# The four score maps of a differential-attention half: PSUM layout and order of their matmuls

## The chip, the cores and the metric

One core of a Trainium2 chip runs the whole program in one launch. The metric is the time of one execution in microseconds of the device (us); lower is better. The kernel's engines are TensorE (PE; its weight loads are listed as PEld), VectorE (DVE), ScalarE (ACT), GpSimd (POOL) and the DMA queues (issued from SyncE, SP).

## The reference

The program is two transformer blocks, two layers each, on 256 tokens of width 1024. Each layer is a feed-forward part, a token mixer and a second feed-forward part. The change lies in the token mixer of the first block, which joins four mixers of four heads each; only differential attention is touched:

```python
def diff_attention(q, k, v, ..., cos, sin):        # 2*DIFF_HEADS = 8 maps, DIFF_DH = 32
    q = apply_rope(q.reshape(bsz, seq, 8, 32), cos, sin)
    k = apply_rope(k.reshape(bsz, seq, 8, 32), cos, sin)
...
        scores = jnp.einsum('bhqd,bhkd->bhqk', q_blk, kt)
        allowed = key_chunk[None, :] <= q_chunk[:, None]      # chunks of 64 tokens
        p = jax.nn.softmax(jnp.where(allowed, scores, -jnp.inf), axis=-1)
        p = p.reshape(bsz, 4, 2, Q_BLOCK, seq)
        return jnp.einsum('bhqk,bhkd->bhqd', p[:, :, 0] - lam * p[:, :, 1], vt)
```

So eight score maps are needed in each of two layers. For the first 128 queries only the first 128 keys can be allowed, for the second 128 all 256: a map is 128 queries by 128 + 256 = 384 keys, with a contraction over 32.

## The kernel before

Each engine has a hand-written order of work, and they meet through counting semaphores: `after(S, name)` waits until the step `name` of the list `S` is done, `then_inc(S.done(name), 1)` counts it. `T1` are TensorE's steps of the mixer, `V1` VectorE's, `A1` ScalarE's.

Every weight matrix is used as a pair of a rounded part and a rest (`w_hi`, made by ScalarE in line 198; `w_lo`, made by VectorE in line 205), in units of 1024 columns, of which three can be held. The mixer of the first block has 16 projections (`project(n)`, lines 229 to 235 and 306 to 312 multiply them), and between them, and halfway through them, TensorE does the small products of the four mixers. One such string of work is a block-wise triangular inverse of twelve steps: `update(i)` (lines 1167 and 1168), then `product(i + 1)` (line 1156) on TensorE, `subtracted(i)` (line 1667) and `masked(i + 1)` (line 1661) on VectorE.

The eight maps are made in two calls, `maps(0)` and `maps(1)`, four maps each. The operand `dqk` holds the 32 features of map j on partitions 32j to 32j + 31, so each matmul uses a quarter of the array's rows, given by `tile_position=(32 * j, 0)`. In PSUM (`ps`, 8 banks of 512 floats) maps 0, 1 and 2 lie in banks 3, 4 and 5, columns 0 to 383 each; map 3 is cut into three pieces of 128 that lie in columns 384 to 511 of the same three banks. Maps 0 to 2 are issued without a wait between them; map 3 waits for the step `map{c}2`. All of this is float32, and a float32 matmul is two passes, each with a weight load and a matmul record in the trace.

TensorE's order is: `update(1)`, `product(2)`, `maps(0)`, first half of projection 9, then `step_2` (`update(2)`, `product(3)`, a wait for `mask_d0`, the row products `rows_m` in line 953), and so on; later `update(3)`, `product(4)`, `maps(1)`, projection 10 with `step_4` halfway (`update(4)`, `product(5)`, a wait for `mask_d1`, the head scores of line 1143, whose two halves `qk_m_even` and `qk_m` also have a wait between them).

On VectorE `masked_maps(c)` waits for `map{c}3`, adds the mask `NEGD` in two instructions while copying the maps from PSUM to `dS` (lines 1681 and 1682), takes the row maxima (line 1686) and scales them (line 1689). ScalarE's `softmax_exp(c)` (line 1472) follows. Then VectorE goes on with `subtracted(2)` or `subtracted(4)`.

Of the kernel before, what the change touches and what calls it, by code (L numbers as in the profile page):

```python
# [22 lines left out]
ALU = mybir.AluOpType  # L23
# [3 lines left out]
P = 128  # L27
SEQ = 256
# [73 lines left out]
def over(ap, shape, *dims):  # L102

    for d in dims:
        ap = ap.unsqueeze(d)
    return ap.to_broadcast(shape)


def build(nc, t, out):
# [8 lines left out]
    def steps(name, names):  # L118
        return Steps(sem(name), names)


    ps = ctx.enter_context(nc.psum_tensor("ps", [P, 8, 512], F32))
# [817 lines left out]
    def scores_T(bank, kT_s, qT_t, h):  # L940

        nc.tensor.matmul(ps[:, bank, 0:SEQ], kT_s[:, 0:P], qT_t[:, 0:SEQ], start=True, stop=True)
        return nc.tensor.matmul(ps[:, bank, SEQ:SEQ + P], kT_s[:, P:SEQ], qT_t[:, P:SEQ], start=True, stop=True)

    def weighted_values(out0, out1, pT, v0, v1):

        nc.tensor.matmul(out0, pT[:, 0:P], v0, start=True, stop=True)
        nc.tensor.matmul(out1, pT[:, P:SEQ], v0, start=True, stop=False)
        return nc.tensor.matmul(out1, pT[:, SEQ:SEQ + P], v1, start=False, stop=True)
# [10 lines left out]
    def diag(buf):  # L960

        return buf[:].rearrange("p h (b n) -> p h b n", b=3)[:, :, 0:3:2, :]
# [72 lines left out]
    dS = m.take(8, 384)  # L1035
# [3 lines left out]
    dqk = rope_in.rearrange("p a (i n) -> p (a i) n", i=2)  # L1039
# [6 lines left out]
    def K(c, n=P):  # L1046
        return con[:, c - NBASE:c - NBASE + n]

    BLOCKS, NEGM, NEGD = K(C_BLOCK), K(C_NEGM), K(C_NEGD, 384)
# [7 lines left out]
    T1 = steps("mix1_t", "narrow sums rows_n kk_even kk qk_even qk x0 rope_t rows_a map00 map01 map02 map03 rows_m map10 map11 "  # L1057
                         "map12 map13 qk_m_even qk_m o_m trans_d vt rows_s xt_s o_d cb o_s u1 l21 transA u2 o_g transB "
                         "transC")
# [48 lines left out]
    def mixer1_pe(pe, B, l, g):  # L1108
        def after(S, name):
            pe.wait_ge(S.sem, S.at(name, l))  # L1110
# [74 lines left out]
            last.then_inc(T1.done(name), 1)  # L1185

        def maps(c):


            for j in range(4):  # L1190
                part = slice(32 * j, 32 * j + 32)
                keys = ((0, slice(0, P)), (P, slice(0, SEQ))) if j < 3 else ((0, slice(0, P)), (P, slice(0, P)), (P, slice(P, SEQ)))
                at = 0
                if j == 3:
                    after(T1, f"map{c}2")
                for i, (t_, s_) in enumerate(keys):
                    o = ps[:, 3 + j, at:at + s_.stop - s_.start] if j < 3 else ps[:, 3 + i, 384:512]
                    at += s_.stop - s_.start
                    last = nc.tensor.matmul(o, dqk[part, c, t_:t_ + P], dqk[part, 2 + c, s_], start=True, stop=True,
                                            tile_position=(32 * j, 0))  # L1200
                last.then_inc(T1.done(f"map{c}{j}"), 1)

        def mix_T(name):
# [102 lines left out]
        for c in range(4):  # L1306
            for tile in range(TILES):
                o = 32 + tile * 8 + 2 * c
                last = nc.tensor.matmul(ps[:, 5, o:o + 2], pm_sq[:, c, tile * P:(tile + 1) * P], BLOCKS[:, 0:P:64],
                                        start=True, stop=True)  # L1310
# [26 lines left out]
        for c in range(4):  # L1337
            for tile in range(TILES):
                o = (c % 2) * SEQ + tile * P
                last = nc.tensor.transpose(ps[:, 3 + c // 2, o:o + P], qkr[:, tile, c * P:(c + 1) * P], IDENT)  # L1340
# [4 lines left out]
        product(2)  # L1345
        after(V1, "mf")
        maps(0)
        project(9, step_2)

        update(3)  # L1350
        product(4)
        after(V1, "dec_m")
        maps(1)
        project(10, step_4)

# [4 lines left out]
        for h in range(H):  # L1360
            last = weighted_values(ps[:, 3, h * 65:(h + 1) * 65], ps[:, 4, h * 65:(h + 1) * 65], dT2[:, h, :],
                                   v_m[:, 0, h, :], v_m[:, 1, h, :])
# [7 lines left out]
        for h in range(H):  # L1370
            for b in range(3):
                last = nc.tensor.transpose(ps[:, 3 + b, h * P:(h + 1) * P], pD[:, h, b * P:(b + 1) * P], IDENT)
# [13 lines left out]
        for grp in range(2):  # L1386
            last = scores_T(3 + grp, cv[:, 8 + grp, :], cv[:, 10 + grp, :], grp)
# [4 lines left out]
        for h in range(H):  # L1392
            last = nc.tensor.matmul(ps[:, 4, h * 64:(h + 1) * 64], lT[:, h, P:SEQ], uu[:, 0, h * 64:(h + 1) * 64],
                                    start=True, stop=True)
# [7 lines left out]
        for h in range(H):  # L1402
            c = slice(h * 64, (h + 1) * 64)
            last = weighted_values(ps[:, 4, h * 64:(h + 1) * 64], ps[:, 4, SEQ + h * 64:SEQ + (h + 1) * 64],
                                   dT[:, h, :], uu[:, 0, c], uu[:, 1, c])
# [237 lines left out]
    def mixer1_dve(v, B, l):  # L1643
        def after(S, name):
            v.wait_ge(S.sem, S.at(name, l))
# [31 lines left out]
        def masked_maps(c):  # L1677

            after(T1, f"map{c}3")
            mine = slice(4 * c, 4 * c + 4)  # L1680
            nc.vector.tensor_tensor(dS[:, 4 * c:4 * c + 3, :], ps[:, 3:6, 0:384], over(NEGD, [P, 3, 384], 1), ALU.add)
            nc.vector.tensor_tensor(dS[:, 4 * c + 3, :].rearrange("p (b n) -> p b n", b=3), ps[:, 3:6, 384:512],
                                    NEGD.rearrange("p (b n) -> p b n", b=3), ALU.add).then_inc(V1.done(f"mask_d{c}"), 1)
            after(V1, f"mask_d{c}")
            for tile, part in enumerate((slice(0, P), slice(P, 384))):
                last = nc.vector.reduce_max(rmax[:, tile, mine], dS[:, mine, part], AX)
            last.then_inc(V1.done(f"max_d{c}"), 1)
            after(V1, f"max_d{c}")
            nc.vector.tensor_scalar(rmax[:, :, mine], rmax[:, :, mine], -(32.0 ** -0.5), None,
                                    ALU.mult).then_inc(V1.done(f"nmax_d{c}"), 1)  # L1690
# [119 lines left out]
        for g_ in range(2):  # L1810
            last = nc.vector.tensor_tensor(X[:, g_, 1, :].rearrange("p (h b n) -> p h b n", h=2, b=2),
                                           diag(lT)[:, 2 * g_:2 * g_ + 2, :, :], over(K(C_MT), [P, 2, 2, P], 1, 1), ALU.mult)
        last.then_inc(V1.done("mt1"), 1)
        after(V1, "mt1")
        for g_ in range(2):
            x4 = X[:, g_, 1, :].rearrange("p (i n) -> p i n", i=4)
            last = nc.vector.scalar_tensor_tensor(x4, x4, -1.0, over(IDENT, [P, 4, P], 1), ALU.mult, ALU.add)
# [9 lines left out]
        for h in range(H):  # L1827
            last = nc.vector.tensor_tensor(sq_m[:, 2 * h:2 * h + 2, :],
                                           ps[:, 3 + h // 2, (h % 2) * SEQ:(h % 2 + 1) * SEQ].rearrange("p (a n) -> p a n", a=2),
                                           over(NEGM, [P, 2, P], 1), ALU.add)  # L1830
# [15 lines left out]

        nc.vector.tensor_scalar(negm, negm, -1.0, 85.0, ALU.mult, ALU.min).then_inc(V1.done("negm"), 1)
        masked_maps(0)
        step(2)
        lo(10, (1,))  # L1850
        after(T1, "rows_m")
        decays(3, 0, dT2, acol, ALU.subtract, ALU.max).then_inc(V1.done("dec_m"), 1)
        step(3)
        lo(11, (0,))
        masked_maps(1)
        step(4)
        lo(11, (1,))
# [31 lines left out]
        for tile, part in enumerate((slice(0, P), slice(P, 384))):  # L1889
            w = part.stop - part.start  # L1890
            last = nc.vector.tensor_tensor(pD[:, :, part], dS2[:, :, 0, part], over(coef[:, tile, 0:8:2], [P, H, w], 2),
                                           ALU.mult)
            last = nc.vector.tensor_tensor(dS2[:, :, 1, part], dS2[:, :, 1, part], over(coef[:, tile, 1:8:2], [P, H, w], 2),
                                           ALU.mult)
# [29 lines left out]
        for grp in range(2):  # L1924
            last = nc.vector.tensor_tensor(dT2[:, 2 * grp:2 * grp + 2, :], over(ps[:, 3 + grp, 0:384], [P, 2, 384], 1),
                                           dT2[:, 2 * grp:2 * grp + 2, :], ALU.mult)
# [72 lines left out]
    part = m2.take(2, SEQ)  # L1999
# [814 lines left out]
```

## Time and profile before

| | |
|---|---|
| median of 3 runs | 2212.68 us (2207.97 to 2214.05) |
| the profiled execution | 2214.05 us, span of its instructions 2212.3 us |
| granted TensorE clock, mean | 0.995 |
| TensorE matmul busy | 2159.8 us, 98% of the span |
| VectorE busy | 1651.9 us, 75% |
| ScalarE busy | 1182.0 us, 53% |
| GpSimd busy | 67.2 us, 3% |
| DMA | 202 GB/s mean |

Busy shares are averages over stages with different limits. Which engine ends last in the mixer is read from the chain of waits and from the timeline of that stage. The profiled execution is the slowest of the three runs, so its sums stand 1.37 us above the median.

### The profile page before, as it was taken

How to read it: one execution, taken by the hardware profiler on the slowest of the kernel's cores; microseconds unless marked ns; L12 is line 12 of the kernel's file. 1: busy time of each engine (PE TensorE's matmuls, PEld its weight loads, DVE VectorE, ACT ScalarE, POOL GpSimd, SP SyncE). 2: the span in 40 equal slices, each digit the busy share in tenths (PEclk: the TensorE clock that was granted, in tenths of full speed). 3: DMA queues.
4: the chain of work that ended last, by engine and by line, in shares of the span. 5: the costliest groups of instructions: out<-in, count | busy, mean ns of one | idle time of the engine just before them, and what ended most of it. 6: DMA issues, size and time to landing. Idle time of an engine off the chain costs nothing.

```text
span 2212.3 us, 34936 instructions
## 1 busy us (share of the span) xinstructions
PE 2159.8 (98%) x13038; PEld 1898.1 (86%) x13038; DVE 1651.9 (75%) x2135; ACT 1182.0 (53%) x1589; POOL 67.2 (3%) x70
## 2 busy tenths in 40 slices
PE   8999999999999999999999999999999999999997
PEld 7888999888888889978888888998888888898886
DVE  6876797778678777867877777768787657766657
ACT  5455535554655573455446546556556545646554
POOL 0000200000000002000000000100000000100000
PEclk9999999999999999999999999999999999999999
DMA  8765322477487642217775775436764555434453
GB/s 308 294 266 210 115 77 95 191 275 286 153 329 270 255 153 96 77 58 286 283 270 211 277 280 203 153 115 235 297 244 174 190 207 209 153 115 152 171 192 150
DMA packets 59414, 446.68 MB, mean 202 GB/s; under 512 B 6976, under 2 KB 7360, under 8 KB 8896
## 3 DMA queue, kind: packets, MB, share of 16 engines
q1 hardware_dynamic: 59328, 445.50, 54.1%
q8 instruction: 59, 0.97, 0.2%
q14 instruction: 27, 0.22, 0.0%
HBM read 444.42 MB, written 1.05 MB: 201 GB/s over the span
## 4 chain that ended last, share of the span: by engine, by line
PE 88%; DVE 6%; ACT 3%; issue 1%; DMA 1%; SPq 0%; DVEq 0%; ACTq 0%
PE ps L248 28%; PE ps L357 15%; PE ps L253 14%; PE ps L363 7%; PE ps L264 3%; PE ps L306 2%; PE ps L307 2%; PE ps L312 2%; PE ps L338 1%; PE ps L229 1%; PE ps L235 1%; PE ps L230 1%; DVE w_lo L205 1%; PE ps L1156 1%; PE ps L1168 1%
## 5 line engine op out<-in xcount | busy, mean ns | idle before, releaser
L205 DVE TENSOR_TENSOR w_lo<-raw,w_hi 128x1024 fp32r<-128x1024 f32 x670 | 812.5, 1233 | 299.7 <-ACT w_hi L198 299.2
L198 ACT ACTIVATE w_hi<-raw 128x1024 fp32r<-128x1024 f32 x670 | 693.9, 1052 | 412.4 <-PE ps L363 133.1
L248 PE MATMUL ps<-hT,w_hi 128*128 128x512 f32 x2688 | 671.3, 392 | 0.1
L248 PEld LDWEIGHTS ps<-hT,w_hi 128*128 128x128 f32 x2688 | 487.9, 189 | 91.0 <-ACT w_hi L198 0.7
L253 PEld LDWEIGHTS ps<-hT,w_lo 128*128 128x128 f32 x2688 | 366.7, 190 | 26.2
L253 PE MATMUL ps<-hT,w_lo 128*128 128x256 f32 x2688 | 374.8, 282 | 0.0
L357 PE MATMUL ps<-w_hi,act_hi 128*128 128x512 f32 x672 | 209.9, 394 | 0.0
L357 PE MATMUL ps<-w_hi,act_lo 128*128 128x512 f32 x672 | 208.3, 391 | 0.0
L363 PE MATMUL ps<-w_lo,act_hi 128*128 128x512 f32 x672 | 179.7, 389 | 0.0
L2048 DVE SCALAR_TENSOR_TENSOR arena<-arena,cond 128x1024 f32<-128x1024 f32 x144 | 168.4, 1219 | 2.3 <-DMA arena<-in_w_ada 2.3
L357 PEld LDWEIGHTS ps<-w_hi,act_lo 128*128 128x128 f32 x672 | 126.7, 189 | 27.7
L363 PEld LDWEIGHTS ps<-w_lo,act_hi 128*128 128x128 f32 x672 | 126.3, 188 | 26.3
L357 PEld LDWEIGHTS ps<-w_hi,act_hi 128*128 128x128 f32 x672 | 121.2, 190 | 20.3
L306 PE MATMUL ps<-w_hi,hT 128*128 128x256 f32 x544 | 137.5, 290 | 0.0
L307 PE MATMUL ps<-w_hi,hT 128*128 128x256 f32 x544 | 133.9, 284 | 0.0
L461 ACT ACTIVATE arena<-ps 128x512 f32<-128x512 f32 x88 | 52.6, 598 | 139.1 <-PE ps L363 117.5
L448 ACT ACTIVATE act_hi<-hidden 128x512 fp32r<-128x512 f32 x80 | 50.5, 631 | 126.3 <-DVE hidden L511 126.3
L508 DVE TENSOR_TENSOR hidden<-ps,arena 128x512 f32<-128x512 f32 x88 | 60.8, 691 | 71.6 <-ACT arena L461 71.5
L306 PEld LDWEIGHTS ps<-w_hi,hT 128*128 128x128 f32 x544 | 104.7, 192 | 1.4 <-issue 0.7
L307 PEld LDWEIGHTS ps<-w_hi,hT 128*128 128x128 f32 x544 | 104.8, 193 | 0.0
L491 DVE TENSOR_TENSOR act_lo<-hidden,act_hi 128x512 fp32r<-128x512 f32 x80 | 55.3, 692 | 55.8 <-ACT act_hi L448 55.8
L453 ACT ACTIVATE arena<-ps 128x512 f32<-128x512 f32 x88 | 52.7, 599 | 78.9 <-PE ps L253 68.8
(364 smaller groups left out, 2535.0 us busy)
## 6 DMA issues: line engine op xcount, KB each, us to landing
raw<-in_u SPq DMA_DIRECT2D x88, 1024.0 KB, 4.9
raw<-in_d SPq DMA_DIRECT2D x88, 1024.0 KB, 6.8
raw<-in_g SPq DMA_DIRECT2D x87, 1024.0 KB, 4.9
arena<-in_w_ada SPq DMA_DIRECT2D x48, 1536.0 KB, 7.5
raw<-in_w_in SPq DMA_DIRECT2D x54, 1024.0 KB, 4.9
raw<-in_w_out SPq DMA_DIRECT2D x16, 1024.0 KB, 4.8
rows<-in_rows SPq DMA_DIRECT2D x12, 1024.0 KB, 9.0
arena<-in_con SPq DMA_DIRECT2D x1, 1344.0 KB, 11.1
```

Of the source, the lines that this page charges most:

```text
L198: nc.scalar.activation(w_hi[:, buf, 0:width], raw[:, slot, half * UNIT:half * UNIT + width], ACT.Copy).then_inc(unit_hi, 1)
L205: nc.vector.tensor_tensor(w_lo[:, buf, 0:width], raw[:, slot, half * UNIT:half * UNIT + width], w_hi[:, buf, 0:width].bitcast(F32), ALU.su ...
L248: nc.tensor.matmul(o, h_[:, k, c], hT[:, :, 4 * half + k, :], start=(half == k == 0), stop=False)
L253: last = nc.tensor.matmul(ps[:, bank + s, 0:SEQ], l_[:, k, c], hT_hi[:, 4 * half + k, :], start=False, stop=(half == 1 and k == 3))
L264: last = nc.tensor.matmul(place(s, z), w[:, k, s * P:(s + 1) * P], hT[:, end, 4 * j + k, :], start=start and k == 0 and (banks == 2 or s = ...
L306: nc.tensor.matmul(o, hT_hi[:, 4 * half + k, c], h_[:, k, :], start=(half == tile == k == 0), stop=False)
L307: nc.tensor.matmul(o, hT_lo[:, 4 * half + k, c], h_[:, k, :], start=False, stop=False)
L357: nc.tensor.matmul(ps[:, 2 * tile + half, :], part[:, c], w_hi[:, buf, half * 512:(half + 1) * 512], start=start and i == 0, stop=False)
L363: last = nc.tensor.matmul(ps[:, 2 * tile + half, :], left[0][:, c], w_lo[:, buf, half * 512:(half + 1) * 512], start=False, stop=stop)
L491: nc.vector.tensor_tensor(home[:, 0:FB // P, :].rearrange("p s t -> p (s t)"), act, hi[:, 0:FB // P, :].rearrange("p s t -> p (s t)").bitc ...
L508: nc.vector.tensor_tensor(out_, in_, part, ALU.add).then_inc(up_sum, 1)
L2048: last = nc.vector.scalar_tensor_tensor(block, block, 1.0, cond[:], ALU.mult, ALU.mult, accum_out=modc[:, n, b:b + 1] if k is first_chunk ...
```

## The change

Map by map, the pieces get another place in PSUM and another order. The 128-column pieces of all four maps (first 128 queries) lie side by side in bank 3. The 256-column pieces (second 128 queries) lie two to a bank in banks 4 and 5. Each map is now two matmuls, also map 3, and each map but the first waits for the one before it. On VectorE the mask is still added in two instructions, now one over the 4 x 128 columns of bank 3 and one over the 4 x 256 columns of banks 4 and 5.

```diff
         def maps(c):
             for j in range(4):
                 part = slice(32 * j, 32 * j + 32)
-                keys = ((0, slice(0, P)), (P, slice(0, SEQ))) if j < 3 else ((0, slice(0, P)), (P, slice(0, P)), (P, slice(P, SEQ)))
-                at = 0
-                if j == 3:
-                    after(T1, f"map{c}2")
-                for i, (t_, s_) in enumerate(keys):
-                    o = ps[:, 3 + j, at:at + s_.stop - s_.start] if j < 3 else ps[:, 3 + i, 384:512]
-                    at += s_.stop - s_.start
-                    last = nc.tensor.matmul(o, dqk[part, c, t_:t_ + P], dqk[part, 2 + c, s_], start=True, stop=True,
-                                            tile_position=(32 * j, 0))
+                if j:
+                    after(T1, f"map{c}{j - 1}")
+                nc.tensor.matmul(ps[:, 3, j * P:(j + 1) * P], dqk[part, c, 0:P], dqk[part, 2 + c, 0:P],
+                                 start=True, stop=True, tile_position=(32 * j, 0))
+                last = nc.tensor.matmul(ps[:, 4 + j // 2, (j % 2) * SEQ:(j % 2 + 1) * SEQ], dqk[part, c, P:SEQ],
+                                        dqk[part, 2 + c, :], start=True, stop=True, tile_position=(32 * j, 0))
                 last.then_inc(T1.done(f"map{c}{j}"), 1)
...
             after(T1, f"map{c}3")
             mine = slice(4 * c, 4 * c + 4)
-            nc.vector.tensor_tensor(dS[:, 4 * c:4 * c + 3, :], ps[:, 3:6, 0:384], over(NEGD, [P, 3, 384], 1), ALU.add)
-            nc.vector.tensor_tensor(dS[:, 4 * c + 3, :].rearrange("p (b n) -> p b n", b=3), ps[:, 3:6, 384:512],
-                                    NEGD.rearrange("p (b n) -> p b n", b=3), ALU.add).then_inc(V1.done(f"mask_d{c}"), 1)
+            nc.vector.tensor_tensor(dS[:, mine, 0:P], ps[:, 3, :].rearrange("p (j n) -> p j n", j=4),
+                                    over(NEGD[:, 0:P], [P, 4, P], 1), ALU.add)
+            nc.vector.tensor_tensor(dS[:, mine, P:384].rearrange("p (b j) n -> p b j n", b=2),
+                                    ps[:, 4:6, :].rearrange("p b (j n) -> p b j n", j=2),
+                                    over(NEGD[:, P:384], [P, 2, 2, SEQ], 1, 1), ALU.add).then_inc(V1.done(f"mask_d{c}"), 1)
```

## Rows read from the trace of the kernel before

**Rows 1.** The page's chain of work that ended last, by engine.
```profile
PE 88%; DVE 6%; ACT 3%; issue 1%; DMA 1%; SPq 0%; DVEq 0%; ACTq 0%
```

**Rows 2.** Line 1199 over the span: durations in ns; then who it waited for (us, times).
```profile
L1199 PE MATMUL ps<-arena x72: 270/372/377, 281.0 to 880.8; 32*128 32x128 f32 x48, 32*128 32x256 f32 x24
  PE ps L1199: 2.2, 4
```

**Rows 3.** Timeline of PE, first call, windows of different width: start, length, instructions.
```profile
280.95 0.40 PE L1199 MATMUL ps<-arena 32*128 32x128 f32 x3
...
281.17 0.52 PE L1199 MATMUL ps<-arena 32*128 32x128 f32 x6
...
281.28 0.62 PE L1199 MATMUL ps<-arena 32*128 32x256 f32 x6
...
281.50 0.40 PE L1199 MATMUL ps<-arena 32*128 32x256 f32 x3
...
282.05 0.93 PE L1199 MATMUL ps<-arena 32*128 32x128 f32 x6
282.91 0.39 PE L306 MATMUL ps<-w_hi,hT 128*128 128x256 f32 x1
```

**Rows 4.** Timeline of PEld, first call, at map 3; idle before it in brackets.
```profile
282.05 0.18 PEld L1199 LDWEIGHTS ps<-arena 32*128 32x128 f32 x1 [0.55 <-PE ps L1199]
```

**Rows 5.** Timeline of PE, the second call, and the fourth with what follows it.
```profile
296.00 2.02 PE L1199 MATMUL ps<-arena 32*128 32x128 f32 x18
...
879.04 2.02 PE L1199 MATMUL ps<-arena 32*128 32x128 f32 x18
880.99 0.39 PE L229 MATMUL ps<-hT,w_hi 128*128 128x256 f32 x1
```

**Rows 6.** Timeline of PE, two narrow windows about the wait inside the head scores.
```profile
305.04 0.27 PE L1143 MATMUL ps<-arena 64*128 64x128 f32 x1
...
305.37 0.37 PE L1143 MATMUL ps<-arena 64*128 64x128 f32 x1
```

**Rows 7.** Timeline of VectorE about the first call's maps.
```profile
281.31 0.68 DVE L1661 TENSOR_TENSOR hidden<-ps,arena 128x512 f32<-128x512 f32 x1
...
283.58 1.35 DVE L1681 TENSOR_TENSOR arena<-ps,arena 128x1152 f32<-128x1152 f32 x1
...
284.85 0.55 DVE L1682 TENSOR_TENSOR arena<-ps,arena 128x384 f32<-128x384 f32 x1
...
287.88 1.22 DVE L1667 TENSOR_TENSOR arena<-arena,ps 128x1024 f32<-128x1024 f32 x1 [0.42 <-PE ps L1168]
```

**Rows 8.** Timeline of PE: the products that ask for the masked maps, both calls.
```profile
288.57 1.95 PE L953 MATMUL ps<-base,arena 128*128 128x128 f32 x16
...
303.71 3.26 PE L1143 MATMUL ps<-arena 64*128 64x128 f32 x24
```

**Rows 9.** Timeline of VectorE about the second call's maps.
```profile
299.86 1.34 DVE L1681 TENSOR_TENSOR arena<-ps,arena 128x1152 f32<-128x1152 f32 x1
301.12 0.54 DVE L1682 TENSOR_TENSOR arena<-ps,arena 128x384 f32<-128x384 f32 x1
...
311.85 1.22 DVE L1667 TENSOR_TENSOR arena<-arena,ps 128x1024 f32<-128x1024 f32 x1 [1.57 <-PE ps L1168]
```

**Rows 10.** Waits of PE over the span, those late in the mixers: us, times, longest.
```profile
PE ps L947 <- issue: 3.1, 2, 1.5
...
PE ps L947 <- ACT arena L1589: 1.2, 2, 0.6
```

**Rows 11.** Windows: length, busy PE, PEld, DVE, ACT, POOL (count), clock, DMA.
```profile
940.00:943.40 3.40, 1.85 (x17) 1.68 (x16) 2.79 (x4) 0.00 (x0) 0.00 (x0) 1.00 0.00 0
943.40:950.20 6.80, 6.80 (x34) 6.80 (x34) 0.46 (x1) 1.81 (x3) 0.00 (x0) 0.50 0.00 0
...
963.90:967.30 3.40, 3.40 (x10) 2.72 (x10) 2.76 (x3) 1.55 (x2) 0.00 (x0) 0.50 0.66 270
...
1950.30:1953.80 3.50, 3.50 (x19) 3.50 (x18) 3.46 (x5) 1.92 (x2) 0.00 (x0) 0.51 0.52 129
```

## The prediction

> **What bounds the kernel now.** I read the chain of work that ended last first. TensorE holds 88% of it, VectorE 6%, DMA 1% [rows 1]: a microsecond added to TensorE's stream is a microsecond of the kernel, unless TensorE waits for somebody later anyway. Then the answers for the changed matmuls' own line, and the timeline around them in windows narrow enough to pull single passes apart. The reader should see two things there. First, line 1199 ran 72 passes, 48 of 128 columns and 24 of 256, in four calls (two in each of two layers), and the only thing it waited for was itself, once in each call, 2.2 us in all [rows 2]. Second, the passes of maps 0, 1 and 2 come in threes: three begin at 280.95 [rows 3]. They lie on different row groups of the array and in different banks, and run side by side.
>
> **The call before, step by step.** The first call starts at 280.95, and the next product behind it (line 306) at 282.91 [rows 3]: 1.96 us. It has two parts.
> - Maps 0 to 2 together. First pass of the 128-column piece at 280.95, second at 281.17, first pass of the 256-column piece at 281.28, second at 281.50 [rows 3]. That is 0.55 us for the four starts. The last three passes take 0.40 us as a group, to 281.90, and map 3 starts at 282.05: the weight load there stood idle for 0.55 us before it, released by line 1199's own matmul [rows 3, 4]. From start to start 1.10 us.
> - Map 3 alone, six passes of 128 columns from 282.05; line 306 follows at 282.91, so 0.86 us [rows 3].
> The fourth call goes from 879.04 to 880.99, 1.95 us [rows 5]; the second begins at 296.00 with the same 18 passes in 2.02 us.
>
> **The call after.** Each map is on its own: two passes of 128 and two of 256 columns. Inside a map nothing changes in speed. The four starts take 0.55 us, since even with three maps side by side each map kept the steps 0.22, 0.11, 0.22 that a lone map shows too: for the lone map 3 the six starts and the tail make 0.86 us. What has to be found is the time from the last pass's start to the next map's first pass, over a wait. Two rows bound it.
> - Upper bound: 0.55 us (281.50 to 282.05), the same shape and row mode, but three matmuls end and signal there, not one, and they begin one after another [rows 3]. With it a map costs 1.10 us.
> - Lower bound: in the head scores one matmul ends and signals. Its last pass starts at 305.04 and the waiting half at 305.37, so 0.33 us, with a 128-column pass [rows 6]. A 256-column pass streams longer by 0.22 - 0.11 = 0.11 us [rows 3], so 0.44 us. With it a map costs 0.99 us.
> I take the lower one, because after the change one matmul signals, as there. Three maps then cost 3 x 0.99 = 2.97 us, and the fourth, followed by the projection without a wait, 0.55 + 0.22 for the last pass + the 0.09 that a change of row mode shows (282.91 less the last 128-column pass's start, which is 282.05 + 0.93 - 0.27 = 282.71, less 0.11), 0.86 us. The call is 3.83 us, 1.87 us longer than before; with the upper bound 3 x 1.10 + 0.86 = 4.16, 2.20 us longer. The matmul saved at map 3 is in this sum already: two steps of 0.11 become one of 0.22, nothing. Four calls: +7.5 us, between +7.3 and +8.8 (I allow 0.2 below the lower bound for starts read to 0.01 us).
>
> The wait between maps is needed for the new layout. The Trainium skill, TensorEngine Tiling, section "Restrictions and Gotchas", says that different row tiles cannot write one PSUM bank at the same time and that software must keep them apart. The trace of before agrees so far as it goes: it shows threes only in three banks. By the rule the threes must go, all of them; were it not a rule and the four maps ran side by side in the new layout, the call would be 0.55 + 0.22 + 0.09 = 0.86 us and the kernel 4.4 us faster, but the new waits exclude that.
>
> The Trainium skill's TensorE: Matmul & The Clock Gate, section on packing small matmuls, adds a tail of about 26 ns for each semaphore increment of concurrent tiles. Three increments against one would be 0.05 us of tail, on the side of the value that I took; the sum above doesn't use it.
>
> **VectorE.** Two instructions over 1152 and 384 elements become two over 512 and 1024, 1536 both times. Before, 1.35 + 0.55 = 1.90 us. The nearest rows, with one operand in PSUM as here, are 0.68 us for 512 and 1.22 us for 1024 [rows 7], 1.90 us. I cost it at nothing; if the pattern over two banks with a repeated mask were slower by a tenth, 0.1 us a call, and hidden as follows. First call: the maps end at 282.98 (282.05 + 0.93) and VectorE began the mask at 283.58. After, they end at 284.85, so the mask starts some 1.3 us later, and so does what is behind it. But `subtracted(2)` at 287.88 had stood idle for 0.42 us waiting for TensorE [rows 7], and TensorE itself comes 1.87 us later: the idle grows to some 1.0 us. TensorE asks for the masked map before the row products at 288.57, 3.2 us after the mask's end at 285.40 [rows 7, 8]; it asks later now. Second call: maps end at 298.02 (296.00 + 2.02), VectorE takes up the mask at 299.86 [rows 5, 9]. In the time shifted by 1.87 us the maps now end at the equivalent of 299.9, so VectorE loses at most 0.1 us there; TensorE's next claim on it, the head scores at 303.71 [rows 8], stands 2.0 us behind the mask's end, 301.66, and VectorE idles 1.57 us for TensorE at 311.85 [rows 9], which takes up the rest. ScalarE's exponentials hang on the maxima and have that same room. No DMA is issued or moved; the weight loads wait for units that come later, not earlier.
>
> **Sum.** 2214.05 + 7.5 = 2221.6 us against the profiled execution; against the median, 1.37 us lower, 2220.2 us, or +0.34%.
>
> **Rivals.**
> - *The delay is taken up late in the mixer.* TensorE waits there in each layer: at line 947, 1.5 us with no releaser shown and 0.6 us for ScalarE, in all 3.1 + 1.2 = 4.3 us [rows 10]. If what it waits for did not hang on TensorE after the maps, 7.5 would shrink to 3.2 us: 2215.9 us, no change that can be told. Against it: VectorE was last idle for TensorE at 311.85 [rows 9], behind both calls, so its chain from there on moves with TensorE's.
> - *Half-clock stretches fall elsewhere.* The granted clock is 0.50 (1.2 GHz of 2.4) in three stretches of 6.8, 3.4 and 3.5 us inside the run; before the first TensorE was busy 1.85 of 3.40 us [rows 11]. Work in them takes twice the time, so they cost 3.4 + 1.7 + 1.75 = 6.85 us. All later work moves by 7.5 us against them; if all vanish the time is 2213.3 us, if one of 6.8 us is added 2223.6 us. This decides for "not slower" once about 1 us of them is saved.
> - *The added waits bring the clock down.* The first half-clock stretch stands behind 3.40 us in which TensorE was busy for 1.85 and otherwise idle in a piece of 1.5 us [rows 10, 11]; the new gaps are of some 0.2 us each, so I doubt it. If each call led to 3.4 us at half clock, 4 x 1.7 = 6.8 us more: 2227.0 us. The Trainium skill's clock page (same title, Part 1) says that a TensorE that is too little busy is put at 1.2 GHz; the trace agrees behind the idle before 943.40 [rows 11], and no row shows it behind gaps as short as these.
> - *The wait costs as in the row with three signals*: +8.8 us, 2221.5 us; the same sign as the forecast.
>
> **How the numbers follow.** The three runs shown lie 6.1 us apart, and a difference under 0.3% (6.6 us) can't be told from none; my +7.5 lies just outside. The forecast's mechanism with +7.3 to +8.8 us has 0.75; taken up late 0.08; half-clock stretches moved in its favour by more than 1 us 0.10; brought down 0.05; something not seen that makes it faster 0.02. Since the forecast itself lies only 0.9 us above the bound and medians move by 2 us, a third of its chance falls within 0.3%. Slower: 0.75 x 0.7 + 0.05 = 0.57. Same: 0.39, faster 0.04. The range goes from 2213.3 (all stretches gone) to 2226, just under the clock rival.
>
> **What would show it.** Right: line 1199 with 64 passes, 32 and 32; no passes in threes; three waits in each call, twelve in all, for itself; call to projection 3.8 to 4.2 us; VectorE's two masks 0.68 and 1.22 us; the wait at line 947 unchanged. Wrong: a call of 3 us or less, waits of line 947 shorter by what the calls gained, or half-clock stretches in other places than in [rows 11].

## The result: 13.6 us slower, nearly half of it through the clock

The kernel after takes 2226.95 us (median of 4 runs, 2225.23 to 2228.34) against 2213.31 us for the kernel before in the same comparison, 13.6 us more. The ratio over all timed runs of the two kernels (eleven of the kernel after) is 1.0068, with a 95% interval of [1.0056, 1.0082]. It is slower, clear of noise, and the median lies 0.95 us above the upper end of the predicted range.

The page of the profiled execution, span and busy time of TensorE, then the chain of work that ended last by engine; the shares are those of [rows 1]:

```profile
span 2225.7 us, 34909 instructions
...
PE 2171.4 (98%) x13019; PEld 1906.2 (86%) x13030; DVE 1653.0 (74%) x2135; ACT 1181.8 (53%) x1589; POOL 67.1 (3%) x70
...
PE 88%; DVE 6%; ACT 3%; issue 1%; DMA 1%; SPq 0%; DVEq 0%; ACTq 0%
```

The new matmuls' own lines, counts and durations in ns, and whom the first of them waited for (us, times), against [rows 2]:

```profile
L1192 PE MATMUL ps<-arena x32: 270/372/575, 279.6 to 893.8; 32*128 32x128 f32 x32
...
  PE ps L1194: 5.8, 12
...
L1194 PE MATMUL ps<-arena x32: 374/377/629, 279.9 to 894.1; 32*128 32x256 f32 x32
```

64 passes, 32 and 32, and twelve waits of TensorE for itself where there were four. Now the first call on TensorE's timeline, against [rows 3]:

```profile
279.57 0.48 PE L1192 MATMUL ps<-arena 32*128 32x128 f32 x2
279.90 0.59 PE L1194 MATMUL ps<-arena 32*128 32x256 f32 x2
280.55 0.48 PE L1192 MATMUL ps<-arena 32*128 32x128 f32 x2
...
282.82 0.59 PE L1194 MATMUL ps<-arena 32*128 32x256 f32 x2
283.35 0.39 PE L306 MATMUL ps<-w_hi,hT 128*128 128x256 f32 x1
```

One map follows another at 0.98 us, and the call takes 283.35 - 279.57 = 3.78 us, 1.82 us more than before. But the maxima of the durations above, 575 and 629 ns, don't fit this call. They come from the second and third. The end of the second call and the start of projection 10:

```profile
298.39 0.48 PE L1192 MATMUL ps<-arena 32*128 32x128 f32 x2
298.72 0.85 PE L1194 MATMUL ps<-arena 32*128 32x256 f32 x2
299.63 0.79 PE L1192 MATMUL ps<-arena 32*128 32x128 f32 x2
300.21 1.06 PE L1194 MATMUL ps<-arena 32*128 32x256 f32 x2
301.20 0.58 PE L229 MATMUL ps<-hT,w_hi 128*128 128x256 f32 x1
301.58 0.41 PE L230 MATMUL ps<-hT,w_hi 128*128 128x256 f32 x1
301.79 0.41 PE L229 MATMUL ps<-hT,w_hi 128*128 128x256 f32 x1
```

From 298.9 on a pair that took 0.59 us takes 1.06, and the projection's passes stand 0.21 us apart instead of 0.12. The windows show the granted clock there (columns as in [rows 11]; these are all the half-clock stretches of the run but the one at its end):

```profile
298.90:305.70 6.80, 6.74 (x27) 5.43 (x27) 5.25 (x6) 0.00 (x0) 0.37 (x1) 0.50 0.01 2
367.20:374.00 6.80, 6.80 (x34) 6.80 (x34) 1.82 (x2) 2.61 (x3) 0.00 (x0) 0.50 0.19 42
875.80:879.20 3.40, 3.40 (x15) 2.87 (x14) 2.73 (x4) 0.00 (x0) 0.00 (x0) 0.50 0.00 0
957.70:964.50 6.80, 6.80 (x33) 6.80 (x33) 1.82 (x2) 2.61 (x3) 0.00 (x0) 0.50 0.00 0
1452.60:1456.00 3.40, 3.40 (x19) 3.40 (x17) 3.02 (x5) 2.36 (x2) 0.00 (x0) 0.50 0.70 217
1964.60:1968.00 3.40, 3.40 (x18) 3.40 (x17) 2.97 (x4) 2.46 (x2) 0.00 (x0) 0.50 0.70 217
```

30.6 us at 0.50 against 13.7 us in [rows 11]. Two of them begin inside calls: the second call runs from 296.44 to 301.20, the third from 872.31 to 876.33.

The 13.4 us between the two spans can be placed by the starts of the four calls. Before they are 280.95, 296.00, 863.99 and 879.04, after 279.57, 296.44, 872.31 and 890.67. From first to second: 16.87 - 15.05 = +1.82 us, a call's direct cost and nothing else. From second to third: 575.87 - 567.99 = +7.88, that is 1.82 and 6.06 more, with two stretches of 6.8 us that the profile of before has not: one begins in the second call, the other lies in the tail of the first layer's mixer. From third to fourth: 18.36 - 15.05 = +3.31, 1.82 and 1.49, with the stretch at 875.8. From the fourth to the end: 1335.03 - 1333.26 = +1.77, a direct cost, with 13.6 us of half clock after and 13.7 us before, the end left out. The first call begins 1.38 us earlier. Together 7.3 us direct and, with that 1.38 us taken off, 6.1 us otherwise.

VectorE, first call, against [rows 7]:

```profile
283.45 0.69 DVE L1676 TENSOR_TENSOR arena<-ps,arena 128x512 f32<-128x512 f32 x1 [1.16 <-PE ps L1194]
284.06 1.22 DVE L1678 TENSOR_TENSOR arena<-ps,arena 128x1024 f32<-128x1024 f32 x1
...
288.31 1.22 DVE L1662 TENSOR_TENSOR arena<-arena,ps 128x1024 f32<-128x1024 f32 x1 [0.98 <-PE ps L1168]
```

Its two masks take 0.69 and 1.22 us, and its idle before `subtracted(2)` grew from 0.42 to 0.98 us: it is later than before, and TensorE later still.

### The profile page after: what moved, and what is told of

Read it like the earlier page. It is cut to its first block, busy times and chain, and to the rows that moved or that the text cites. A ratio compares the mean times of both kernels' runs of the same rounds, so it can differ in the third digit from the quotient of the medians.

```text
span 2225.7 us, 34909 instructions
## 1 busy us (share of the span) xinstructions
PE 2171.4 (98%) x13019; PEld 1906.2 (86%) x13030; DVE 1653.0 (74%) x2135; ACT 1181.8 (53%) x1589; POOL 67.1 (3%) x70
## 4 chain that ended last, share of the span: by engine, by line
PE 88%; DVE 6%; ACT 3%; issue 1%; DMA 1%; SPq 0%; DVEq 0%; ACTq 0%
PE ps L248 27%; PE ps L357 15%; PE ps L253 14%; PE ps L363 7%; PE ps L264 3%; PE ps L306 2%; PE ps L307 2%; PE ps L312 2%; PE ps L229 1%; PE ps L338 1%; PE ps L230 1%; PE ps L235 1%; DVE w_lo L205 1%; PE ps L1156 1%; PE ps L1168 1%
## 5 line engine op out<-in xcount | busy, mean ns | idle before, releaser
L306 PE MATMUL ps<-w_hi,hT 128*128 128x256 f32 x544 | 141.9, 297 | 0.0
L307 PE MATMUL ps<-w_hi,hT 128*128 128x256 f32 x544 | 137.8, 289 | 0.0
L306 PEld LDWEIGHTS ps<-w_hi,hT 128*128 128x128 f32 x544 | 108.1, 199 | 2.1 <-issue 1.6
L307 PEld LDWEIGHTS ps<-w_hi,hT 128*128 128x128 f32 x544 | 108.1, 199 | 0.0
```

What stands on the lines that cost most here:

```text
L306: nc.tensor.matmul(o, hT_hi[:, 4 * half + k, c], h_[:, k, :], start=(half == tile == k == 0), stop=False)
L307: nc.tensor.matmul(o, hT_lo[:, 4 * half + k, c], h_[:, k, :], start=False, stop=False)
```

## The experiments

Two theories stood at the start. **A**: maps one at a time cost directly, and bring the clock down at the calls. **B**: the layout or VectorE's form has a part. Then, within A, what it is that brings the clock down: **G**, the gaps of the waits, or **R**, a stretch in which one quarter of the array's rows works alone. A granted clock of 0.50 is called half clock. In all that follows "direct" is four times what a call at full clock takes over 1.95 us.

**The waits alone, old layout** (`waits_only`).

```diff
-                if j == 3:
-                    after(T1, f"map{c}2")
+                if j:
+                    after(T1, f"map{c}{j - 1}")
```

> The kernel before with one edit: every map waits for the one before it (as after the change); PSUM places, map 3 in three pieces and VectorE's masks stay as before. Theory A (the waits do it all: their gaps take about 1.8 us a call, and they also bring the granted clock down behind some of the calls): 7.3 us at full clock for four calls plus half-clock stretches, 12 to 15 us slower than before, half-clock stretches behind calls of line 1199. Theory B (the layout or VectorE's new form has a part): clearly less than that, 7 to 8 us slower, no new half-clock stretch.

Measured 2226.14 us, 13.5 us over before, ratio 1.0067 [1.0054, 1.0080]. The fourth call, the one at full clock, takes 3.78 us. Half-clock stretches begin in the other three, the last of them at its very end (279.96 to 284.67, 299.78 to 304.08, 872.66 to 876.45):

```profile
282.50:289.30 6.80, 6.74 (x29) 5.98 (x28) 3.98 (x6) 0.00 (x0) 0.00 (x0) 0.50 0.09 36
303.00:309.80 6.80, 6.80 (x33) 6.58 (x33) 4.50 (x6) 0.19 (x1) 0.00 (x0) 0.50 0.01 2
876.40:879.80 3.40, 3.40 (x17) 3.35 (x16) 3.21 (x4) 0.00 (x0) 0.00 (x0) 0.50 0.00 0
```

The whole loss is there without the new layout. Theory B falls.

**The new layout with three row groups side by side** (`threes_new`): `wide(j)` and `short(j)` are the two matmuls of a map as after the change.

```diff
+            for k in range(2):
+                if k:
+                    after(T1, f"map{c}1")
+                wide(k)
+                wide(2 + k)
+                short(1 - k).then_inc(T1.done(f"map{c}{2 * k}"), 1)
+                after(T1, f"map{c}{2 * k}")
+                short(3 - k).then_inc(T1.done(f"map{c}{2 * k + 1}"), 1)
```

> The kernel after with its layout and VectorE's two masks kept, but the matmuls in another order: the wide pieces of two maps and the short piece of a third side by side in three banks, three waits a call, about 2.1 us a call instead of 3.8. Theory A (one map at a time, with gaps, is what costs, directly and through the clock): within 2 us of the kernel before, half-clock stretches only in the tail of the mixer as before. Theory B (layout): stays near the time after, some 5 us faster at most by its shorter calls.

Measured 2216.80 us, 4.1 us over before, ratio 1.0021 [1.0012, 1.0031]; more than I allowed. A call takes 2.52 us, not 2.1, so 2.3 us are direct. The runs reach from 2210.7 us (clock 0.997) to 2220.7 us (0.992), and the profile has one stretch of 6.8 us, at 360.0 in the tail of the first layer's mixer, that those of the kernel before don't have. At the calls the granted clock is 1.00, all four of them:

```profile
276.00:300.00 24.00, 23.55 (x196) 21.10 (x195) 20.86 (x31) 9.18 (x24) 2.35 (x1) 1.00 0.26 89
863.00:888.00 25.00, 24.55 (x204) 22.10 (x203) 21.82 (x32) 9.19 (x25) 2.35 (x1) 1.00 0.26 85
```

So the layout can be had for 9.5 us less than the kernel after pays.

**Waits spread over dense work** (`scattered`), before's maps untouched:

```diff
                     token_unit(pe, B, j, 6 + n % 2, half)
+                if 5 <= n <= 11:
+                    pe.wait_ge(unit_done, B + (j + 1 + CREDIT))
```

> The kernel before with its maps untouched, and TensorE made to wait for its own last product behind each of 14 weight units of projections 5 to 11, in both layers: 28 gaps of about 0.22 us, 6.2 us of direct cost, spread one to each 4 us of dense work. If what brings the clock down is gaps that stand close together (8 waits and maps alone in 4 us), it is 6 to 7 us slower than before and has no half-clock stretch in the stretch of projections 5 to 11. If any added wait in this part of the mixer does it, 10 to 16 us slower, with half-clock stretches there.

Measured 2219.92 us, 7.2 us over before, ratio 1.0040 [1.0027, 1.0053]. Both windows over the whole of that part of the mixer stand at full clock:

```profile
250.00:330.00 80.00, 78.88 (x657) 74.43 (x656) 63.99 (x91) 25.50 (x56) 10.23 (x10) 1.00 0.23 75
840.00:915.00 75.00, 73.88 (x612) 69.43 (x612) 59.60 (x83) 25.31 (x56) 7.54 (x6) 1.00 0.21 71
```

28 spread waits cost about the time expected of them (6.2 us) and no clock there. Both G, for gaps close together, and R allow this.

**Each map's matmuls twice** (`twice`): `for _ in range(2):` around the two matmuls of a map.

> The kernel after with the two matmuls of each map issued twice to the same place: the same waits and gaps, but 1.30 us of passes for each gap instead of 0.65. Direct cost against the kernel after 16 x 0.65 = 10.4 us. If the gaps' share of the time is what brings the clock down, the half-clock stretches behind the calls go, and it is only 5 to 8 us slower than the kernel after (18 us slower than before); if the gaps as such do it, 10 us slower than after (24 us slower than before).

Measured 2250.27 us, 37.6 us over before, ratio 1.0171 [1.0154, 1.0187]. That is beyond both expectations: 10.4 us more work made it 24 us slower than the kernel after, each against the runs of before beside it. The stretches at the four calls grew:

```profile
284.50:291.30 6.80, 6.80 (x29) 6.06 (x28) 3.81 (x5) 0.00 (x0) 0.00 (x0) 0.50 0.01 2
305.00:315.20 10.20, 10.14 (x38) 8.39 (x38) 4.26 (x6) 0.00 (x0) 0.00 (x0) 0.50 0.00 0
881.80:892.00 10.20, 10.08 (x37) 8.28 (x37) 3.81 (x5) 0.00 (x0) 0.00 (x0) 0.50 0.00 0
905.70:915.90 10.20, 10.08 (x36) 8.01 (x35) 4.74 (x6) 0.00 (x0) 0.00 (x0) 0.50 0.00 0
```

The gaps' share of the call is smaller here, and the loss larger. This turned me to R, and the next four kernels were made for it.

**The waits kept, all rows at work** (`fullrows`); the maps are sums over four heads:

```diff
-                part = slice(32 * j, 32 * j + 32)
+                part = slice(0, P)
...
-                                 start=True, stop=True, tile_position=(32 * j, 0))
+                                 start=True, stop=True)
```

> The kernel after with the same waits and gaps, but each map's matmuls contract over all 128 partitions, the full height of the array, instead of 32 (so the maps are sums over four heads, not the reference's). Theory R (rows): direct cost as after, 7 us over the kernel before, and no half-clock stretch behind the calls: 2219 to 2221 us. Theory G (gaps): 2226 us like the kernel after, with half-clock stretches behind calls.

Measured 2218.46 us, 7.6 us over before (2210.84 us in this comparison), ratio 1.0035 [1.0024, 1.0046]. The waits are all there, 5.5 us of weight-load idle in twelve, against 5.8 in the kernel after. A call is 3.41 us, 5.8 us direct. It is 0.37 us shorter than in the kernel after, and the pitch of two maps in the middle of it is the same 0.98 us; the difference lies at its ends, where the kernel after changes the row mode. The clock stands:

```profile
276.00:303.00 27.00, 26.65 (x206) 24.14 (x205) 23.02 (x33) 9.30 (x25) 2.35 (x1) 1.00 0.24 79
862.00:889.00 27.00, 26.65 (x206) 24.15 (x205) 23.03 (x33) 9.35 (x25) 2.35 (x1) 1.00 0.24 79
```

**No waits, one row group** (`onegroup`): all four maps are taken from the first 32 partitions (maps 1 to 3 repeat map 0), which need not wait for each other.

```diff
-                part = slice(32 * j, 32 * j + 32)
-                if j:
-                    after(T1, f"map{c}{j - 1}")
+                part = slice(0, 32)
...
-                                 start=True, stop=True, tile_position=(32 * j, 0))
+                                 start=True, stop=True, tile_position=(0, 0))
```

> The kernel after without its waits: all four maps are taken from the first 32 partitions and the first row group (maps 1 to 3 repeat map 0's numbers), so no two row groups meet and nothing has to wait. No gap is left; a call is 4 x 0.65 + 0.2 = 2.8 us, 0.85 us more than before, 3.4 us in all. Theory R (rows): half-clock stretches behind calls still, 5 to 8 us slower than before. Theory G (gaps): none, 3 to 4 us slower.

Measured 2221.06 us, 10.2 us over before, ratio 1.0049 [1.0036, 1.0063], for a direct cost of 3.4 us (a call is 2.81 us). TensorE's third and fourth call, without a gap, and the clock behind them:

```profile
864.50:867.30 2.80, 2.80 (x17) 2.29 (x16) 2.66 (x7) 0.00 (x0) 0.00 (x0) 1.00 0.94 331
868.20:871.60 3.40, 3.40 (x18) 3.40 (x18) 3.04 (x4) 0.00 (x0) 0.00 (x0) 0.50 0.00 0
881.90:884.70 2.80, 2.80 (x17) 2.28 (x16) 2.80 (x3) 0.49 (x2) 2.33 (x1) 1.00 0.00 0
885.30:888.70 3.40, 3.40 (x19) 3.40 (x18) 3.37 (x5) 0.00 (x0) 0.00 (x0) 0.50 0.00 0
```

PE busy 2.80 of 2.80 us, and half clock 0.6 to 0.9 us later. The first two calls had no stretch; but the profiled run was the fastest of the five (2217.62 us, clock 0.994, the others 0.990 to 0.993), so 2 of 4 may be low for this kernel. G falls on both sides: gaps without a drop, a drop without gaps.

**The same, each matmul twice** (`onegroup2`).

> The same with each matmul issued twice: no gap, one row group at work for 8 x 0.65 + 0.2 = 5.4 us a call, 3.45 us more than before, 13.8 us in all. Theory R: half-clock stretches at all or nearly all four calls, 20 to 35 us slower than before. Theory G: none at the calls, 14 us slower.

Measured 2240.03 us, 29.2 us over before, ratio 1.0136 [1.0120, 1.0151], for 13.9 us direct (5.43 us a call at full clock). Half-clock stretches begin in or right behind all four calls, at 283.4, 307.3, 880.7 and 904.6.

**Full rows, each matmul twice** (`fullrows_twice`), the counterpart of `twice`.

> The kernel of the run twice (each matmul of a map issued two times, waits kept), contracting over all 128 partitions instead of 32 (the maps are sums over four heads). A call is 3.41 us as with full rows once, and 2.6 us for the second round of passes, 6.0 us: 4.05 us over before, 16.2 us in all. Theory R (a quarter of the rows alone brings the clock down): 16 to 19 us slower than before, no half-clock stretch at the calls. If long calls or waits did it: near the 37.6 us of the run twice.

Measured 2233.75 us, 22.6 us over before (2211.13 us), ratio 1.0102 [1.0085, 1.0119]: 15 us less than `twice`, but 3.6 us over what I expected. All four calls take the same 6.03 us, and the clock stands at them:

```profile
276.00:310.00 34.00, 33.65 (x254) 30.72 (x252) 24.19 (x35) 11.76 (x32) 2.36 (x1) 1.00 0.19 63
868.00:903.00 35.00, 34.66 (x261) 31.74 (x261) 25.68 (x38) 10.53 (x26) 2.36 (x1) 1.00 0.19 61
```

Its stretches lie elsewhere, two of 6.8 us in the tails of the two layers' mixers and two of 3.4 us in the second block:

```profile
368.30:375.10 6.80, 6.80 (x34) 6.80 (x34) 1.82 (x2) 2.61 (x3) 0.00 (x0) 0.50 0.19 31
962.20:969.00 6.80, 6.80 (x34) 6.80 (x34) 1.82 (x2) 2.61 (x3) 0.00 (x0) 0.50 0.08 13
```

The kernel before has them in the second layer's tail and once in the second block [rows 11], in its other profile too. So the miss is of some weight: 22.6 - 16.3 = 6.3 us over the direct cost is as much as in the kernel after, and none of it arises at the calls. R tells where the 15 us to `twice` went, but not what these 6.3 us are; whether a longer call moves later work into half clock or this is chance, these runs leave open.

**The maps spread through a projection** (`interleaved`): `between(i)` issues map i ahead of every fourth pass of the unit's first part.

```diff
+                if between and k % 2 == 0:
+                    between(2 * s + k // 2)
...
-        maps(0)
-        project(9, step_2)
+        project(9, step_2, maps(0))
```

> The kernel after with the four maps of a call spread through the first unit of projection 9 or 10, four passes of the projection between two maps: the same waits in the program, but nothing idle in them; instead the array changes its row mode twice for each map. By the rows each map then costs 0.65 us of passes and about 0.3 us for the two mode changes and the first loads, 3.8 us a call as in the kernel after. Theory R (a stretch in which one quarter of the rows works alone brings the clock down): no half-clock stretch at the calls, 7 to 9 us slower than before, 5 us faster than after. Theory of the direct cost alone (the clock falls by chance of place): like the kernel after, 13 us slower than before.

Measured 2221.73 us, 10.9 us over before, ratio 1.0040 [1.0026, 1.0054], with runs from 2216.0 to 2227.7. A call with its 12 passes of the projection between takes 5.39 us (3.95 without them), 8.0 us direct. In the profile two of four calls still had a half-clock stretch (874.6 and 895.1), so the expectation of none was wrong. That profile is of the slowest of the five runs (clock 0.991, the others 0.994 to 0.997), and the kernel stands 2.7 us less over before than the kernel after does, at a direct cost that is 0.7 us higher: thinned out, the maps cost less through the clock, and probably bring it down less often.

**Both kernels once more** (`after_again`, `before_again`).

> The kernel after unchanged, one more profile. Theory R: again at least one half-clock stretch that begins in or right behind a call of lines 1192 and 1194, perhaps at other calls than in the first profile; 2225 to 2231 us. If the first profile's places were chance: none at the calls.

> The kernel before unchanged, one more profile. Theory R: no half-clock stretch at the calls of line 1199, some in the tails of the mixers and the second block, 2207 to 2216 us.

2228.51 us and 2213.22 us. In the second profile of the kernel after all four calls have a stretch (they start at 279.28, 297.64, 870.44 and 890.34):

```profile
283.10:286.50 3.40, 3.40 (x17) 3.40 (x17) 3.30 (x4) 0.00 (x0) 0.00 (x0) 0.51 0.02 5
300.20:307.00 6.80, 6.74 (x28) 5.60 (x27) 5.15 (x6) 0.00 (x0) 0.26 (x1) 0.50 0.01 2
873.60:880.40 6.80, 6.80 (x30) 6.15 (x30) 3.81 (x5) 0.16 (x1) 0.00 (x0) 0.50 0.00 0
894.10:897.50 3.40, 3.40 (x17) 3.39 (x17) 3.37 (x5) 0.00 (x0) 0.00 (x0) 0.50 0.00 0
```

In the second profile of the kernel before none has:

```profile
276.00:300.00 24.00, 23.70 (x208) 22.42 (x208) 21.36 (x31) 9.29 (x24) 2.37 (x1) 1.00 0.27 89
860.00:884.00 24.00, 23.70 (x209) 22.42 (x209) 21.37 (x32) 9.91 (x25) 2.37 (x1) 1.00 0.26 89
```

All of it in one table; the clock is the median of the runs' mean granted clocks.

| kernel | rows at work in a call | direct us | measured us over before | beyond direct | clock | calls with half clock |
|---|---|---|---|---|---|---|
| before, twice profiled | three quarters, then one | 0 | 0 | 0 | 0.995 to 0.996 | 0 of 8 |
| threes_new | three quarters, one | 2.3 | 4.1 | 1.8 | 0.994 | 0 of 4 |
| scattered | as before | not in the calls | 7.2 | | 0.995 | 0 of 4 |
| fullrows | all, with waits | 5.8 | 7.6 | 1.8 | 0.995 | 0 of 4 |
| fullrows_twice | all, with waits | 16.3 | 22.6 | 6.3 | 0.993 | 0 of 4 |
| interleaved | one quarter, thinned | 8.0 | 10.9 | 2.9 | 0.994 | 2 of 4 |
| onegroup | one quarter, no waits | 3.4 | 10.2 | 6.8 | 0.992 | 2 of 4 |
| waits_only | one quarter, waits | 7.3 | 13.5 | 6.2 | 0.992 | 3 of 4 |
| after, twice profiled | one quarter, waits | 7.3 | 13.6 | 6.3 | 0.991 | 6 of 8 |
| onegroup2 | one quarter, no waits | 13.9 | 29.2 | 15.3 | 0.989 | 4 of 4 |
| twice | one quarter, waits | 17.7 (3.78 + 4 x 0.65 a call, worked out) | 37.6 | 19.9 | 0.985 | 4 of 4 |

## Why the prediction was wrong

**Right: what bounds the kernel, and the direct cost.** TensorE's stream sets the time; a map cost 0.98 us (forecast 0.99), a call 3.78 (3.83), four calls +7.3 us (+7.5). Taking the lower bound for the wait was right. The first call to the second, free of half clock, grew by 1.82 us to the hundredth.

**Right: what is hidden.** VectorE's masks took 0.69 + 1.22 us as costed, and its idle in front of `subtracted(2)` grew to 0.98 us (forecast 1.0). The wait at line 947 is the same 3.1 us in two as in [rows 10]: nothing was taken up late, and that rival falls.

**Wrong: "The added waits bring the clock down", given 0.05.** This is the step that failed. The sum put the clock at nothing, and the range ended at 2226 us, just under this rival's 2227.0. I rejected it because the new gaps are short, and compared its stretch only with one in which TensorE stood idle in a piece. Measured, the excess over the direct cost is 13.6 - 7.3 = 6.3 us. Both profiles show half-clock stretches in other places than [rows 11], which was my own sign of being wrong. The clock was lower in all five runs of `waits_only` and in every run of the kernel after (0.990 to 0.992 in eleven runs; before 0.994 to 0.997 in the 17 timed beside `waits_only`). That the rival's price of 6.8 us comes so near is partly luck: it stood for 3.4 us of half clock at each call, while the first profile has 10.2 us at two calls and 6.8 us in a mixer's tail, and the second 20.4 us at four.

Its mechanism was wrong as well. `fullrows` has the same waits and no drop at a call, `onegroup` has no wait and drops. What the change took away was not only time between matmuls but three row groups at work together. In the six profiles in which one quarter of the rows works alone through a call (2.81 us at the shortest), half clock began in a call or within 0.9 us behind it 19 times in 24; in the six with three quarters or all at work, never in 24. The runs leave open what about the quarter-height matmuls it is. A full-height one differs in its row mode too, and no kernel here keeps three groups side by side for as long as 2.8 us (a call of `threes_new` is 2.52 us), so the time spent in that mode is not set apart from the rows at work in it. `interleaved`, whose maps stand alone for 0.65 us each and which still drops at two calls, points to no unbroken stretch being needed.

The page that I cited beside that rival (the Trainium skill, TensorE: Matmul & The Clock Gate, Part 1) puts the drop down to how busy TensorE was. By the profile's busy row TensorE was busy all through `onegroup`'s calls, 2.80 of 2.80 us, and the clock fell behind two of them. The busy row alone did not tell the drop here; the measurement decides.

**A reading that was too wide.** I wrote that by the rule on PSUM banks "the threes must go, all of them". `threes_new` keeps the new layout and has three groups side by side in three banks; only a fourth at the same time has no bank of its own. That order costs 4.1 us where the kernel after costs 13.6.

**Half-clock stretches elsewhere.** I had listed this with 0.10 as a gain. In the profile of the kernel after it was a loss in the first layer's tail (367.2, part of the 6.06 us between second and third call) and even behind the fourth call. Five of the eleven profiles of changed kernels have a stretch in that tail (`threes_new`, `fullrows_twice`, `onegroup2`, `interleaved` and the first of the kernel after), the two of the kernel before have none. Such stretches also come and go between runs of one kernel: the 17 runs of before beside `waits_only` lie 7.8 us apart, the fastest at a clock of 0.997 and the slowest at 0.994.

**Where the 1.82 us of a call come from.** `onegroup` splits them: one map at a time without waits is 2.81 us, 0.86 us over before; the three waits add 3.78 - 2.81 = 0.97 us, 0.32 us each. Half is lost concurrency, half the waits. Nothing run here beats the kernel before.

## What to carry to other kernels

When a change takes matmuls on partial row groups from side by side to one at a time, price two things: the passes that no longer overlap with their waits, which rows of the trace give to some hundredths, and the clock behind the stretch, which here cost nearly as much again. Look at the granted clock around the place, not only at TensorE's busy time, since a TensorE busy to 100% on a quarter of its rows was followed by half clock. If a layout forces row groups into one bank, order the matmuls so that others go to other banks at the same time; in `threes_new` that was worth 9.5 us.

## What the runs showed that I had not expected

- In `threes_new` the wait for a short matmul lasted until the wide ones issued ahead of it were over. The short one's second pass would have been done 0.48 us after its start; the next short one began only 0.78 us after it:

```profile
279.38 0.48 PE L1195 MATMUL ps<-arena 32*128 32x256 f32 x2
279.39 0.48 PE L1190 MATMUL ps<-arena 32*128 32x128 f32 x2
279.70 0.38 PE L1195 MATMUL ps<-arena 32*128 32x256 f32 x2
280.17 0.48 PE L1190 MATMUL ps<-arena 32*128 32x128 f32 x2
```

  The wide passes end at 280.08. That makes the call 2.52 us where I had worked out 2.1. The Trainium skill says that matmuls start and end in program order (TensorE: Matmul & The Clock Gate, the section on packing small matmuls); this agrees.
- Going into the row mode of a quarter and out of it again cost about as much as a wait (0.32 us): in `interleaved`, a map with its four passes of projection took 1.52 us, 0.39 us more than the 0.65 + 0.48 us of passes.
- 10.4 us of quarter-row passes added to the kernel after cost 24 us (13.6 to 37.6 over before); 10.5 us of full-row passes added to `fullrows` cost 15 us (7.6 to 22.6).
